# Turning normalized rows by a product with a diagonal instead of normalizing them first

## The reference

```python
def _rmsnorm(x):
    xf = x.astype(jnp.float32)
    y = xf * lax.rsqrt(jnp.mean(xf * xf, axis=-1, keepdims=True) + NORM_EPS)
    return y.astype(x.dtype)

def _modulate(x, shift, scale):
    return _rmsnorm(x) * (1 + scale[:, None, :]) + shift[:, None, :]
...
    for i in range(DEPTH):
...
        h = _modulate(x, sh_a, sc_a)
...
        x = x + g_a[:, None, :] * m
        h = _modulate(x, sh_f, sc_f)
```

## Time and profile before

| | us |
|---|---|
| median of 3 runs | 1817.58 (1816.38 to 1818.53) |
| the profiled execution, its own time | 1818.67 |
| its span in the profile | 1816.80 |
| TensorE busy | 1551.3 (85%) |
| VectorE busy | 1260.1 (69%) |
| ScalarE busy | 848.6 (47%) |

### The profile page before, as it was taken

The page is one execution under the profiler, slowest core; times in us unless marked ns, Lnnn a source line. Parts: engine busy times, 40 slices in busy tenths (PEclk is TensorE's granted clock), DMA queues, the critical chain, the costliest instruction groups (busy, mean ns, idle before and its releaser), DMA issues.

```text
span 1816.8 us, 21972 instructions
## 1 busy us (share of the span) xinstructions
PE 1551.3 (85%) x7718; PEld 1258.9 (69%) x7718; DVE 1260.1 (69%) x1629; ACT 848.6 (47%) x1175; POOL 42.3 (2%) x53
## 2 busy tenths in 40 slices
PE   3799879999698996999856999489999999999993
PEld 1787659777596675999745667367777776777772
DVE  7767549664686337787845223478988988988885
ACT  0534444344333223343233111167767777776773
POOL 0000000000000000000000000000000000000001
PEclk9989898999897577999977557589999999999997
DMA  9755328351495005677731002177897897797792
GB/s 400 279 187 207 119 79 309 133 207 70 171 348 199 0 24 208 256 280 291 284 114 43 5 0 93 51 274 290 344 391 313 335 400 313 317 420 312 317 407 82
DMA packets 60521, 403.12 MB, mean 222 GB/s; under 512 B 6422, under 2 KB 9622, under 8 KB 13980
## 3 DMA queue, kind: packets, MB, share of 16 engines
q1 hardware_dynamic: 52416, 379.48, 53.5%
q10 hardware_dynamic: 6012, 15.30, 2.3%
q0 software_dynamic: 2016, 7.34, 1.1%
HBM read 393.18 MB, written 8.91 MB: 221 GB/s over the span
## 4 chain that ended last, share of the span: by engine, by line
PE 55%; DVE 24%; ACT 7%; DMA 6%; issue 6%; POOL 1%; SPq 1%; DVEq 0%; ACTq 0%; POOLq 0%
DVE w_lo L1761 13%; PE PS L743 12%; PE PS L745 12%; PE PS L744 12%; DMA raw<-in_ws 6%; PE PS L842 5%; ACT w_hi L1314 3%; PE PS L863 3%; PE PS L852 2%; ACT xg L1441 2%; DVE acc L1778 1%; PE PS L973 1%; PE PS L953 1%; PE PS L830 1%; PE PS L813 1%
## 5 line engine op out<-in xcount | busy, mean ns | idle before, releaser
L1761 DVE TENSOR_TENSOR w_lo<-raw,w_hi 128x2048 fp32r<-128x2048 f32 x287 | 657.8, 2292 | 152.7 <-ACT w_hi L1314 127.3
L1314 ACT ACTIVATE w_hi<-raw 128x2048 fp32r<-128x2048 f32 x287 | 548.6, 1920 | 290.7 <-PE PS L745 240.3
L743 PE MATMUL PS<-w_hi,h_hi 128*128 128x512 f32 (+2 forms) x812 | 335.6, 413 | 33.7 <-DVE w_lo L1761 14.0
L744 PE MATMUL PS<-w_lo,h_hi 128*128 128x512 f32 (+2 forms) x812 | 318.9, 393 | 0.0
L745 PE MATMUL PS<-w_hi,h_lo 128*128 128x512 f32 (+2 forms) x812 | 318.7, 393 | 0.0
L743 PE MATMUL PS<-h_hi,w_hi 128*128 128x256 f32 x776 | 230.7, 297 | 27.2 <-DVE h_lo L1806 17.7
L744 PE MATMUL PS<-h_lo,w_hi 128*128 128x256 f32 x776 | 225.5, 291 | 0.0
L745 PE MATMUL PS<-h_hi,w_lo 128*128 128x256 f32 x776 | 225.1, 290 | 0.0
L743 PEld LDWEIGHTS PS<-w_hi,h_hi 128*128 128x128 f32 x812 | 156.4, 193 | 81.7 <-DVE w_lo L1761 27.7
L1778 DVE SCALAR_TENSOR_TENSOR acc<-raw,cs,acc 128x512 f32<-128x512 f32 x252 | 189.5, 752 | 8.9
L745 PEld LDWEIGHTS PS<-w_hi,h_lo 128*128 128x128 f32 x812 | 156.1, 192 | 32.7
(11 more groups left out here) (296 smaller groups left out, 1652.9 us busy)
## 6 DMA issues: line engine op xcount, KB each, us to landing
raw<-in_ws SPq DMA_DIRECT2D x359, 1024.0 KB, 6.2
y_rows<-ysb ACTq DMA_DIRECT2D x10, 512.0 KB, 8.4
rp<-in_rp ACTq DMA_DIRECT2D x1, 3072.0 KB, 11.6
ckb<-in_ck ACTq DMA_DIRECT2D x2, 1024.0 KB, 4.7
y_rows<-ones ACTq DMA_DIRECT2D x3, 512.0 KB, 9.5
x<-in_x SPq DMA_DIRECT2D x1, 1024.0 KB, 11.3
gpost<-in_gpost ACTq DMA_DIRECT2D x2, 512.0 KB, 5.1
x_rows<-xn_f ACTq DMA_DIRECT2D x2, 512.0 KB, 2.8
```

What stands on the lines that cost most here:

```text
L743: t.matmul(out, lhs[0], rhs[0], start=start, stop=False, skip_group_check=True)
L744: t.matmul(out, lhs[0], rhs[1], start=False, stop=False, skip_group_check=True)
L1314: a.activation(wh[:, SPL_AT[e.phase][i], :], raw[:, r, :], ACT.Copy).then_inc(*e.inc("hi"))
L1761: v.tensor_tensor(wl[:, s, :], raw[:, r, :], wh[:, s, :].bitcast(F32), ALU.subtract).then_inc(*e.inc("raw_used"))
```

## The change

VectorE no longer writes x times the reciprocal norm before the turn. It multiplies the 128 x 128 identity by the reciprocal norms of a tile of tokens and so writes a diagonal matrix, once for each tile (diag). TensorE then forms, for each piece, the ordinary f32 product of x (as weights) with that diagonal: the result is the turned piece, each token scaled. Tile diag lies where pt lies, a buffer of the attentions that is free at this time. `turn` remains for nao and mo, without its second argument, which it never used.

In rt the normalized rows are still wanted in HBM. VectorE writes them to xn_f after all of h_lo, and ScalarE's two DMAs to x_rows move behind `h_hi(0)`.

```diff
@@ build @@
+        diag = nc.alloc_sbuf_tensor_at("diag", [P, MT, P], F32, offset=at[0] - 2 * S * 4)
@@ tensor engine @@
+            def turn_x():
+
+                for b in range(4):
+                    for k in range(2):
+                        for m in range(MT):
+                            kt = 2 * b + k
+                            c = (k * 2 + m) * P
+                            last = t.matmul(PS[:, 4 + b, c:c + P], x[:, m, kt * P:(kt + 1) * P], diag[:, m, :],
+                                            start=True, stop=True)
+                    last.then_inc(*e.inc("turned"))
+
...
-                pe.wait_ge(*e.at("xn", 2))
-                turn(xn_l, 0)
+                pe.wait_ge(*e.at("diag", 2))
+                turn_x()
                 feat_slot(0, LAY_BANK[0:2], fresh=True)
...
@@ scalar engine, rt @@
             a.activation(wrh[:], pcol("router"), ACT.Copy).then_inc(*e.inc("router_hi"))
+            h_hi(0)
             for m in range(MT):
                 act.wait_ge(*e.at("xn", m + 1))
                 act.dma_start(x_rows[m * P:(m + 1) * P, :], xn_f[:, m, :]).then_inc(*e.inc("saved", 16))
-            h_hi(0)
             act.wait_ge(*e.at("router_t", 1))
@@ vector engine @@
-            def norm(xn, wa, wb):
+            def norm(wa, wb):
 
                 dve.wait_ge(*e.at("rstd", 1))
                 for m in range(MT):
-                    v.tensor_scalar(xn[:, m, :], x[:, m, :], st[:, s_rs + m:s_rs + m + 1], None,
-                                    ALU.mult).then_inc(*e.inc("xn"))
-                    dve.wait_ge(*e.last("xn"))
+                    v.tensor_scalar(diag[:, m, :], ident, st[:, s_rs + m:s_rs + m + 1], None,
+                                    ALU.mult).then_inc(*e.inc("diag"))
+                    dve.wait_ge(*e.last("diag"))
@@ vector engine, rt @@
-            norm(xn_f, ab[:, 0, :], ab[:, 1, :])
+            norm(ab[:, 0, :], ab[:, 1, :])
+            for m in range(MT):
+                v.tensor_scalar(xn_f[:, m, :], x[:, m, :], st[:, s_rs + m:s_rs + m + 1], None,
+                                ALU.mult).then_inc(*e.inc("xn"))
+                dve.wait_ge(*e.last("xn"))
```

More of the change, by code:

```diff
@@ L197 @@
     "cscores": {"lay": 1},
+    "diag": {"lay": 2, "na": 2, "ffn": 2, "mla": 2, "rt": 2},
     "down_used": {"mla": 2},
@@ L269 @@
     "x_turned": {"go": 1, "moe": 1, "more": 1},
-    "xn": {"lay": 2, "na": 2, "ffn": 2, "mla": 2, "rt": 2},
+    "xn": {"rt": 2},
     "y": {"pre": 1, "lay": 4},
@@ L821, in ada, with turn @@
                 last.then_inc(*e.inc("ada_sum"))
-            def turn(src, stage):
+            def turn_x():
[7 more added lines that the diff above has]
+                    last.then_inc(*e.inc("turned"))
+            def turn(src):
                 for b in range(4):
@@ L1211, in _ @@
             used.clear()
-            pe.wait_ge(*e.at("xn", 2))
-            turn(xn_n, 0)
+            pe.wait_ge(*e.at("diag", 2))
+            turn_x()
             pe.wait_ge(*e.at("h", 4))
@@ L1225, in _ @@
             pe.wait_ge(*e.at("o_used", 4))
-            turn(nao, 1)
+            turn(nao)
             out_proj(12)
@@ L1230, in _ @@
             used.clear()
-            pe.wait_ge(*e.at("xn", 2))
-            turn(xn_f, 0)
+            pe.wait_ge(*e.at("diag", 2))
+            turn_x()
             pe.wait_ge(*e.at("h", 4))
@@ L1237, in _ @@
             used.clear()
-            pe.wait_ge(*e.at("xn", 2))
-            turn(xn_m, 0)
+            pe.wait_ge(*e.at("diag", 2))
+            turn_x()
             pe.wait_ge(*e.at("h", 4))
@@ L1276, in _ @@
             pe.wait_ge(*e.at("o_used", 4))
-            turn(mo, 1)
+            turn(mo)
             out_proj(5)
@@ L2071, in layer @@
                 make_ab(1, LP["bcol"], LP["gpre"])
-                norm(xn_l, ab[:, 0, :], ab[:, 1, :])
+                norm(ab[:, 0, :], ab[:, 1, :])
                 dve.wait_ge(*e.at("gpost", 1, 16))
@@ L2289, in _ @@
             make_ab(1, pcol("bcol", 0, 16))
-            norm(xn_n, ab[:, 0, :], ab[:, 1, :])
+            norm(ab[:, 0, :], ab[:, 1, :])
             for s in range(6):
@@ L2319, in _ @@
             make_ab(1, pcol("bcol", 32, 48))
-            norm(xn_m, ab[:, 0, :], ab[:, 1, :])
+            norm(ab[:, 0, :], ab[:, 1, :])
             split_to(3)
```

## The result

The changed kernel takes 1823.36 us (median of 13 runs, 1821.44 to 1825.77) against 1817.58 of the kernel before (13 runs, 1815.41 to 1819.38). The ratio is 1.0032, with a 95% interval of 1.0024 to 1.0041: 5.8 us slower. The profiled execution took 1825.36 us with a span of 1823.5, 6.7 more than the span before.

A forecast was written before the change was run, and what follows sets the result against it. No single engine bounds the kernel; each stage's serial chain does. Each boundary moves 1.70 - 0.94 = +0.77 us; four full shifts (3.1) plus 0.8 for the layers give +3.9, so 1821.5 us, range 1815.0 to 1825.5.

The forecast's parts named there:

- the forecast's own range: Whole kernel: +2.4 us if half-speed stretches end when they do today, to +5.5 with six full shifts; forecast's chance 0.52.
- rival (b): First products in na, mla and router: later start meets a later clock rise, +3.4 us more, hence +7.3; chance 0.17.
- Where the chain leaves TensorE: At each boundary: at bank 1, after eight transposes, because h_hi of bank 0 stands behind ScalarE's scaling of bank 1.
- The multiplications, -0.94: At each boundary: two 128x128 multiplications of 0.286 us replace two of 0.754 us, gaining 0.94 us on the chain.
- The product is two records of a transpose's cost: Turning up to bank 1: 16 records where it took 8, 0.213 us each, 1.70 us more per boundary.
- (c): At each boundary: a product with a diagonal costs one transpose, giving 0.94 us back, -5.6 us in all; chance 0.06.
- (d): At each boundary: a product's records are dearer than a transpose's, +2.0 us each, +12 us in all; chance 0.03.
- The other banks do not end it: At each boundary: banks 2 and 3 are turned before they are asked for, with about a microsecond of slack.
- The router's moves cost nothing: Router stage: moved multiplications (1.54 us) fit VectorE's idle time; x_rows land nearly 9 us before the gather. Cost nothing.
- The worth by stage: na, ffn, mla and router each pass on 0.77 us, 3.1 together; lay1 +0.5 and lay0 +0.3; sum +3.9 us.
- Rival (a): na, mla, router: clock raised by longer turning holds to first products, saving up to 1.9, 2.1, 1.8 us; total -2.5; chance 0.20.

The follow-up runs named there:

- the second execution: The same changed kernel, unedited, profiled once more: 1825.71 us, against 1825.36 us in its first profiled execution.
- the last kernel: Kernel before with ScalarE copying h_hi before scaling bank 1, normalized rows in two halves, 36 idle transposes in na, mla and rt: 1807.49 us, ratio 0.9943.
- changed kernel, h_hi first: Changed kernel with ScalarE writing h_hi of bank 0 before it scales bank 1: 1818.06 us, ratio 0.9997 to the kernel before.
- with 40 transposes: Changed kernel plus 40 idle transposes of the identity behind the turning products of na, mla and rt: 1817.36 us, ratio 0.9997 to the kernel before.

## Why the prediction was right, and where it was short

It said 1821.5, slower, 1815.0 to 1825.5; measured were 1823.4 and slower. The 5.8 us lie above the forecast's own range of +2.4 to +5.5 and inside the stated one only because that reached up to rival (b)'s +8. The path and both prices hold; that the total came so near is in part luck, because the stages' worth was not what it summed. By its own steps:

- **Where the chain leaves TensorE: right.** It leaves at bank 1, after 16 records where it was 8. Turning ScalarE's order round moved the leaving point to bank 2 and gave back 5.3 us, so the reason given, ScalarE's queue, holds too.
- **The multiplications, -0.94: right.** diag takes 0.286 us, and alone they gave 0.93 at every boundary.
- **The product is two records of a transpose's cost: right in number, the term a little too small.** +1.70 was forecast, +1.82 measured, so that the boundary moves by 0.88 and not by 0.77. The spacing of 0.213 us was right from the second record on. What the sum left out is the first record: the second starts 0.375 us behind it, with transposes 0.265, and the longest record of the turn takes 583 ns where it took 474. These 0.11 us and 8 x 0.213 are the 1.82. The 3.7 us forecast to ScalarE's first scaling were 3.8, and na's first product came 11.25 us (480.91 to 492.16) behind the first turning record, where 11.1 was said. Rivals (c), a product for the price of a transpose, and (d), a dearer one, are out.
- **The other banks do not end it: right.** Bank 2's last record ends at 486.3 and VectorE scales it at 487.10, when its h_lo is done; bank 3 ends at 487.2 and ScalarE scales it at 489.05. Nothing beside the 0.88 shows up in any wait.
- **The router's moves cost nothing: right.** Timeline of after, as the earlier trace rows:

```profile
1155.96 1.54 DVE L2399 TENSOR_SCALAR xn_f<-x,st 128x1024 f32<-128x1024 f32 x2
1156.74 1.12 ACTq L1743 DMA_DIRECT2D x_rows<-xn_f  x2
...
1162.55 0.17 DVE L2406 COPY rw<-PS 128x16 f32<-128x16 f32 x1 [5.05 <-PE PS L1307]
...
1171.95 1.19 POOL L704 DMA_INDIRECT xt<-x_rows,token_of  x1 [27.94 <-DVE token_of L2006]
```

  VectorE still idles 5.05 us before the logits, and the gather is released by token_of, not by x_rows, 14 us after the last issue.
- **The worth by stage: here the prediction was short.** It summed four full shifts and 0.8 for the layers. Measured against before, in the first and the second execution: lay0 +0.24 and +0.78, lay1 +2.30 and +0.12, na +1.04 in both, ffn +0.44 and +0.43, mla +0.18 and +2.34, from the router on +2.6 and +2.5.
- In ffn, where the whole 0.88 was counted, the product of the earlier trace rows still has it: it comes at 723.57, 35.00 us behind the mark, before at 719.19, 34.11 behind. The half was lost later. VectorE's rows behind the stage's two later stretches at half speed, first of before, then of after:

```profile
726.79 2.29 DVE L1761 TENSOR_TENSOR w_lo<-raw,w_hi 128x2048 fp32r<-128x2048 f32 x1 [5.77 <-ACT w_hi L1314]
918.89 0.69 DVE L1900 TENSOR_TENSOR scaled_y<-PS,gate 128x512 f32<-128x512 f32 x1 [12.03 <-PE PS L745]
```

```profile
730.98 2.29 DVE L1775 TENSOR_TENSOR w_lo<-raw,w_hi 128x2048 fp32r<-128x2048 f32 x1 [5.57 <-ACT w_hi L1328]
922.82 0.69 DVE L1914 TENSOR_TENSOR scaled_y<-PS,gate 128x512 f32<-128x512 f32 x1 [11.85 <-PE PS L748]
```

  Against the marks (685.08 and 688.57) the first is 0.70 late, the second 0.44. The two stretches at half speed ended 39.65 and 230.80 us behind the mark before and 39.93 and 231.08 after: 0.28 later, while the program was 0.88 and 0.70 later. So less of the program lay in them, and they gave back 0.18 and 0.26 us. That the clock's position did this is read from these rows; no run set it by itself.
- In the layers VectorE's second w_lo comes 0.88 to 0.89 later against its mark in both (66.52 for 65.72, and 279.95 for 278.91, with marks 0.09 earlier and 0.16 later), where about 0.8 was forecast. In mla the first products' stretch at half speed ended 3.1 us behind the first product and not 4.1, and 28 us behind the mark the program was 0.44 late. From the router on, 1.6 of the first execution's 2.6 came by the first gather (28.64 us behind the power instead of 27.06), of which 0.83 is the wait and the rest the longer stretch at half speed, 6.0 us behind the first product for 3.8 before. In the second execution, where it was 3.8, the gather came 0.88 late; there the other 1.6 us, and in the first about 1.0, came in the experts' rounds, and I cannot say why.
- **The whole.** The six boundaries by 0.88 are 5.3 us, less what ffn swallows (0.44) 4.8, and the two profiles have 1.9 and 2.2 us beyond that (spans 6.7 and 7.0 longer). The forecast's 3.9 would have been 4.6 with the right term (0.11 six times). The rest up to the 5.8 measured is not split into causes; the clock's position (lay1, mla, the router) and the unexplained part of the experts' rounds lie in it.
- **Rival (a), the clock holds on: its mechanism is real, its place was not.** In na, ffn, mla and the router the first products began at 0.50, after 4.9 to 5.7 us of idle TensorE. Where the gap was closed by other work, the changed kernel gained about 6 us, the size of (a)'s 5.8, and the kernel before 2 to 3. In the layers (a)'s condition was met: lay1's first products ran at 0.50 for 3.4 us before and at 1.00 from the start after (gap 2.4 us), and in lay0 21 records start in 4.30 us before (61.3 to 65.6) and 25 in 2.98 after (61.8 to 64.8). Yet lay0 was 0.2 and lay1 2.3 us longer in that execution, lay1 with the later stretches at half speed shown with the second execution.
- **Rival (b), a later rise behind the first products: in one of eight places.** In na, ffn, mla and the router the level came back 4.2, 3.3, 3.1 and 6.0 us behind the first product, before 3.8, 3.9, 4.1 and 3.8; in the second execution 4.2, 3.3, 3.1 and 3.8. So (b) held for the router in the first execution and cost 0.75 us there, and in ffn and mla the stretch became shorter.
- **The Trainium skill** (TensorE: Matmul & The Clock Gate, Part 4, PE-mode transpose) has transposes not count as a busy TensorE. The trace disagreed before, and the experiments settle it for these f32 transposes: in the last kernel all that TensorE did between na's norm and its first product were transposes, the granted clock rose from 0.50 to 1.00 at 477.65 among them, and that product and those behind it ran at 1.00 (483.40 to 487.40, above).

What stays open: that the clock took back the shorter waits of two kernels is read from where the level fell and rose, in one profile of each. No experiment set those places by itself, so it is argued, not shown. Shown is that the same waits with the level held at the first products of na, mla and the router are 9 us faster (0.9943 against 0.9997); how much of this is the first products and how much the stretches further on is not split.

## What to carry to other kernels

A scale that is folded into an f32 turn makes an ordinary product of each transpose, two records for one. Here the turn was on the chain and cost 1.82 us where the smaller multiplications saved 0.93, so it did not pay, however much work it took off VectorE. Before costing a step with several parts, ask after which part the next engine really starts; here the order of ScalarE's stream decided that, and turning two of its entries round gave the changed kernel back what the change cost; in the kernel before it shortened the waits as well and the time not at all. Where TensorE idles some microseconds before a stage's first products, look at the granted clock behind the gap: shortening the wait and filling the gap gave 10 us together, while the first alone gave nothing.

## What was not expected of the hardware

- Transposes alone kept the granted clock at 1.00. Behind idle gaps of TensorE of up to 1.7 us the first products of na, mla and the router had 1.00 and kept it in all four kernels that had such gaps (0.56 to 1.66 us). Behind 2.3 to 3.0 us they lapsed within 1.2 us or had 0.50 in five of six cases. Behind 4.3 us (changed kernel, h_hi first) they lapsed within 0.9 us, and behind 4.9 us and more, in all kernels looked at, they had 0.50.
- In the layers the length of the gap alone did not decide. Behind 1.87 us lay1's first products lost the level within 0.5 us (changed kernel again, and with 40 transposes), and behind 2.43 us (changed kernel, first execution) and 2.62 us (xn turned by ordinary products) they kept it for over 35 us.
- 88.7 us at half speed in the middle of na became 92.2 us in four of the other kernels and 95.6 in four, though none of them changes an instruction there. An edit may so go with another clock 100 us behind it.
- Two executions of one kernel differed by 2.2 us in a stage, with opposite signs in two stages, while the totals were 0.4 us apart (1825.36 and 1825.71).
- With 3.1 us less waiting a kernel was slower by 2.6 us (1.0014, interval 1.0005 to 1.0023).
